# Feed-forward layers with five plain groups ahead of the seven-product ones, the scaled x split chunk by chunk, and x reloaded in eight parts

## The reference

```python
D_MODEL, D_FF, EPS = 1024, 2816, 1e-6

def swiglu_half(x, g_pre, w_gate, w_up, w_down, g_post):
    h = rmsnorm(x, g_pre)
    y = (jax.nn.silu(h @ w_gate) * (h @ w_up)) @ w_down
    return x + 0.5 * rmsnorm(y, g_post)

xp = swiglu_half(xp, *ffn1)
xp, sp = token_mixing(xp, None, None, buf0, s0, mix)
xp = swiglu_half(xp, *ffn2)      # and the same for the sample tokens xs
```

## Time and profile before

| | us |
|---|---|
| median of 3 runs | 1514.76 (1513.25 to 1514.83) |
| profiled execution | 1506.69 |
| its span, first to last instruction | 1504.8 |
| TensorE busy | 1435.8 (95%), 12096 products |
| VectorE busy | 908.2 (60%) |
| ScalarE busy | 611.1 (41%) |
| POOL busy | 194.1 (13%) |
| mean granted clock of TensorE | 0.986 |

### The profile page before, as it was taken

One profiled execution on the slowest core, in us unless ns is written; L12 is line 12 of the kernel. 1 busy time (PEld: TensorE's weight loads), 2 busy tenths in 40 slices (PEclk: granted clock), 3 DMA queues, 4 the chain that ended last, 5 costly groups with the idle time before them and its releaser, 6 DMA issues. The chain is left out here.

```text
span 1504.8 us, 30863 instructions
## 1 busy us (share of the span) xinstructions
PE 1435.8 (95%) x12096; PEld 1316.4 (87%) x12096; DVE 908.2 (60%) x1475; ACT 611.1 (41%) x1054; POOL 194.1 (13%) x185
## 2 busy tenths in 40 slices
PE   7799999999999999999998999989987999999996
PEld 6699999999898888877876887779987999999996
DVE  7999997222656775243566533456378899993224
ACT  5465655222521454211134333342344556553222
POOL 4400000000171000332100220021016000000000
PEclk9899999999999999999999999989999999999998
DMA  4233222422589979999997567837231223324221
GB/s 146 71 112 113 96 101 94 161 96 86 199 293 350 334 243 320 355 333 343 375 331 265 189 221 248 285 127 260 95 128 71 78 92 113 113 84 160 96 96 57
DMA packets 114846, 275.74 MB, mean 183 GB/s; under 512 B 15721, under 2 KB 18410, under 8 KB 113698
## 3 DMA queue, kind: packets, MB, share of 16 engines
q1 hardware_dynamic: 108050, 249.66, 47.7%
q0 software_dynamic: 6240, 23.28, 4.4%
q10 hardware_dynamic: 432, 1.05, 0.2%
HBM read 257.55 MB, written 16.39 MB: 182 GB/s over the span
## 5 line engine op out<-in xcount | busy, mean ns | idle before, releaser
L201 ACT ACTIVATE w_high<-w_raw 128x1024 fp32r<-128x1024 f32 (+1 forms) x93 | 108.0, 1162 | 451.9 <-PE psum L226 406.5
L205 DVE TENSOR_TENSOR w_low<-w_raw,w_high 128x1024 fp32r<-128x1024 f32 (+1 forms) x93 | 126.9, 1365 | 234.2 <-ACT w_high L201 234.2
L1168 PE MATMUL psum<-h_high,gu_high 128*128 128x260 f32 x608 | 173.8, 286 | 6.6 <-DVE h_low L920 5.6
L1169 PE MATMUL psum<-h_low,gu_high 128*128 128x260 f32 x608 | 173.4, 285 | 0.0
L1170 PE MATMUL psum<-h_high,gu_low 128*128 128x260 f32 x608 | 173.0, 284 | 0.0
L1168 PE MATMUL psum<-sums_high,gu_high 128*128 128x260 f32 x456 | 130.5, 286 | 15.7 <-DVE gu_low L992 12.7
L222 PE MATMUL psum<-mix_h_high,w_high 128*128 128x260 f32 x672 | 139.2, 288 | 0.0
L224 PE MATMUL psum<-mix_h_low,w_high 128*128 128x260 f32 x672 | 135.3, 283 | 0.0
L226 PE MATMUL psum<-mix_h_high,w_low 128*128 128x260 f32 x672 | 135.2, 283 | 0.0
L1170 PE MATMUL psum<-sums_high,gu_low 128*128 128x260 f32 x456 | 129.9, 285 | 0.0
L222 PE MATMUL psum<-a_high,w_high 128*128 128x260 f32 x616 | 124.6, 283 | 3.5 <-DVE w_low L205 3.5
(11 more groups left out here) (448 smaller groups left out, 3314.1 us busy)
## 6 DMA issues: line engine op xcount, KB each, us to landing
kv_ring<-in_cache_k SPq DMA_DIRECT2D x256, 256.0 KB, 4.1
kv_ring<-in_cache_v SPq DMA_DIRECT2D x256, 256.0 KB, 3.8
w_raw<-in_w_dn SPq DMA_DIRECT2D x32, 704.0 KB, 4.1
w_raw<-in_w_proj SPq DMA_DIRECT2D x44, 512.0 KB, 6.7
raw_even<-in_w_gu SPq DMA_DIRECT2D x40, 512.0 KB, 4.3
raw_odd<-in_w_gu SPq DMA_DIRECT2D x40, 512.0 KB, 3.7
spill<-h_f POOLq DMA_DIRECT2D x20, 260.0 KB, 5.0
gates<-spill POOLq DMA_DIRECT2D x16, 260.0 KB, 4.4
```

Source lines behind the costliest of these rows:

```text
L201: act.activation(w_high[:, u, 0:nk, :], w_raw[:, u, 0:nk, :], ACT.Copy).then_inc(high_done, 1)
L205: dve.tensor_tensor(w_low[:, u, 0:nk, :], w_raw[:, u, 0:nk, :], w_high[:, u, 0:nk, :].bitcast(F32), ALU.subtract).then_inc(low_done, 1)
L1168: pe.matmul(out, wh[:, slot, :], hi, start=start, stop=False, skip_group_check=True)
L1169: pe.matmul(out, wh[:, slot, :], lo, start=False, stop=False, skip_group_check=True)
```

## The change

- G0 is 5: groups 0 to 4 are plain, 5 to 21 seven-product. The buffers of the plain groups' weights alternate (odd_high and even_high, and so for low), and t4 takes t1's place. `second_products` runs u = 0 to 7.
- POOL's four additions are gone. ScalarE writes the even chunks of xw as x times the weights with four copies behind the factor (`weighted`), and POOL multiplies by the factor. The orders of ScalarE, VectorE and POOL around the start of the seven-product groups are written anew.
- In the last plain half (u = 7) TensorE counts gu_used after every chunk (the "free" units). `token_high(k)` waits for chunk k alone and not for the whole half.
- In the down stage x comes back in eight transfers, of one chunk each, between those of w_dn blocks 3 and 14; the last three go together.

```diff
 SLOTS = 25
 
 
-G0 = 3
+G0 = 5
 NG7 = KF - G0
 
 
 def unit_order():
 
-    order = [("gate", 1), ("up", 1), ("gate", 2), ("up", 2), ("P5", G0), ("PA", G0), ("P6", G0), ("P7", G0)]
+    order = [(kind, c) for c in range(1, G0 - 1) for kind in ("gate", "up")] + [("gate", G0 - 1)]
+    order += [("free", k) for k in range(KD - 1)] + [("up", G0 - 1), ("P5", G0), ("PA", G0), ("P6", G0), ("P7", G0)]
     for n in range(G0 + 1, KF):
         order += [("PA", n), ("P3", n - 1), ("P5", n), ("P6", n), ("P4", n - 1), ("P7", n)]
...
+POOL_STEPS = [("xw", k) for k in range(0, KD, 2)] + [("late", 0), ("t", 0), ("late", 1), ("t", 1), ("t", 2), ("t", 3)]
+POOL_STEPS += [("late", c) for c in range(2, G0)]
 ACT_STEPS, DVE_STEPS = act_steps(), dve_steps()
 ACT_AT, DVE_AT, POOL_AT = [{t: i + 1 for i, t in enumerate(s)} for s in (ACT_STEPS, DVE_STEPS, POOL_STEPS)]
 
...
                     load(4, 0)
                     load(4, 1)
                     for n in range(5, KF):
-                        sp.wait_ge(gu_dve, V("S4", n - 2))
+                        sp.wait_ge(gu_dve, V("S4", n - 2) if n - 2 >= G0 else V("second", 2 * (n - 3) + 1))
                         load(n, 0)
-                        sp.wait_ge(gu_dve, V("P4", n - 2))
+                        if n - 2 >= G0:
+                            sp.wait_ge(gu_dve, V("P4", n - 2))
                         load(n, 1)
 
                     sp.wait_ge(gu_dve, V("P4", LAST - 1))
                     load_block(sp, w_dn, 0, nb, 0, NKD)
                     sp.wait_ge(gu_used, at("PA", LAST))
                     load_block(sp, w_dn, 1, nb + 1, 1, NKD)
-                    sp.wait_ge(gu_dve, V("low", LAST))
-                    sp.dma_start(x[:, :, :], a["x"] if which == 0 else a["x_spill"]).then_inc(x_back, 16)
-                    load_stream(sp, w_dn, 2 * KD, nb, NKD, first=False)
+                    for n in range(2, 2 * KD):
+                        if n == 4:
+                            sp.wait_ge(gu_dve, V("low", LAST))
+                        if n >= 4 and n % 2 == 0:
+                            for k in range(n // 2 - 2, n // 2 - 1 if n < 2 * KD - 2 else KD):
+                                sp.dma_start(x[:, k, :], a["x"][:, k, :] if which == 0 else a["x_spill"][:, k, :]
+                                             ).then_inc(x_back, 16)
+                        load_block(sp, w_dn, n, nb + n, n % 2, NKD)
                     if which == 0:
                         load_first(sp, a["w_proj"], nb + 2 * KD, KD)
                     if store:
...
 
                     def normed(k):
 
-                        pool.wait_ge(gu_pool, G("add", k))
+                        pool.wait_ge(gu_act, A("xg", k))
                         pool.tensor_tensor(xw[:, k, :], xw[:, k, :], factor[:, :], ALU.mult).then_inc(gu_pool, 1)
 
-                    for k in range(0, KD, 2):
-                        pool.wait_ge(h_low_done, m0 + k + 1)
-                        pool.tensor_tensor(xw[:, k, :], h_high[:, k, :].bitcast(F32), h_low[:, k, :].bitcast(F32),
-                                           ALU.add).then_inc(gu_pool, 1)
                     pool.wait_ge(norm_rec, norm_n + 1)
                     for k in range(0, KD, 2):
                         normed(k)
+                    late(0)
                     pool.wait_ge(gu_pool, G("xw", KD - 2))
                     pool.tensor_tensor(t1[:, :, :], xe1, xe2, ALU.subtract).then_inc(gu_pool, 1)
-                    late(0)
+                    late(1)
                     pool.wait_ge(gu_dve, V("xw", KD - 1))
                     pool.wait_ge(gu_pool, G("t", 0))
                     pool.tensor_tensor(t2[:, :, :], xo2, t1[:, :, :], ALU.add).then_inc(gu_pool, 1)
-                    late(1)
                     pool.wait_ge(gu_pool, G("t", 1))
+                    pool.wait_ge(gu_dve, V("t", 0))
                     pool.tensor_tensor(t4[:, :, :], xo1, t2[:, :, :], ALU.subtract).then_inc(gu_pool, 1)
                     pool.tensor_tensor(xe2, xo2, xe2, ALU.subtract).then_inc(gu_pool, 1)
-                    late(2)
+                    for c in range(2, G0):
+                        late(c)
 
                 @block.scalar
                 def _(act):
...
 
                     def second_high(u):
 
-                        if u < 2:
-                            act.wait_ge(gu_in[2 + u], arrived(1))
-                            src = c_raw[:, u, :, :]
-                        else:
-                            act.wait_ge(gu_in[u - 2], arrived(2))
+                        c, m = u // 2 + 1, u % 2
+                        act.wait_ge(gu_in[2 * (c % 2) + m], arrived(c))
+                        if c == 2:
                             act.wait_ge(gu_dve, V("second", 1))
-                            src = raws[0][:, u - 2, :, :]
-                        act.activation(c_high[u // 2][:, u % 2, :, :], src, ACT.Copy).then_inc(gu_act, 1)
+                        elif c > 2:
+                            act.wait_ge(gu_used, at("up", c - 2))
+                        src = c_raw[:, m, :, :] if c == 1 else raws[c % 2][:, m, :, :]
+                        act.activation(c_high[(c - 1) % 2][:, m, :, :], src, ACT.Copy).then_inc(gu_act, 1)
+
+                    def weighted(k):
+
+                        act.activation(xw[:, k, :], x[:, k, :], ACT.Copy, scale=vecs[:, v_pre + k:v_pre + k + 1]
+                                       ).then_inc(gu_act, 1)
                     second_high(0)
                     second_high(1)
                     factor_act(act, norm_n)
...
                         act.activation(h_high[:, k, tok], xw[:, k, tok], ACT.Copy).then_inc(gu_act, 1)
 
                     def unit_high(kind, n):
...
                         act.wait_ge(gu_dve, V("hid2", n))
                         act.activation(a_high[:, n, :], af[:, :], ACT.Copy).then_inc(gu_act, 1)
 
+                    weighted(0)
+                    weighted(2)
+                    weighted(4)
+                    weighted(6)
                     second_high(2)
                     silu(0)
                     second_high(3)
+                    high(0)
                     silu(1)
-                    high(0)
                     sum_high(0, t_hi[:, 0:4, :], t1[:, :, :])
+                    second_high(4)
                     high(1)
+                    second_high(5)
                     sum_high(1, t_hi[:, 4:8, :], t2[:, :, :])
+                    sum_high(2, t_hi[:, 8:12, :], t4[:, :, :])
+                    silu(2)
+                    high(2)
+                    second_high(6)
+                    second_high(7)
                     act.wait_ge(block_used, n0 + 2)
                     unit_high("PA", G0)
                     unit_high("P5", G0)
-                    sum_high(2, t_hi[:, 8:12, :], t4[:, :, :])
                     unit_high("P6", G0)
-                    silu(2)
-                    act.wait_ge(gu_used, at("up", 2))
+                    silu(3)
+                    high(3)
+                    silu(G0 - 1)
+                    act.wait_ge(gu_pool, G("xw", KD - 2))
                     act.wait_ge(gu_dve, V("xw", KD - 1))
                     for k in range(KD):
                         token_high(k)
                     sum_high(3, T3_HIGH, xe2)
-                    high(2)
+                    high(G0 - 1)
                     if which == 1:
-                        act.wait_ge(x_back, 32 + 16 * KD)
+                        act.wait_ge(x_back, 16 + 32 * KD)
                     second_product(G0)
                     unit_high("PA", G0 + 1)
                     for n in range(G0, KF):
...
                     normed(5)
                     normed(7)
                     second_low(3)
-                    gate_scale(1)
                     hidden(0)
                     low(0)
+                    gate_scale(1)
+                    second_low(4)
                     sum_low(0, t_lo[:, 0:4, :], t1[:, :, :], t_hi[:, 0:4, :])
                     hidden(1)
                     low(1)
+                    second_low(5)
+                    sum_low(1, t_lo[:, 4:8, :], t2[:, :, :], t_hi[:, 4:8, :])
+                    dve.wait_ge(gu_act, A("t", 2))
+                    dve.tensor_tensor(t_lo[:, 8:10, :], t4[:, 0:2, :], t_hi[:, 8:10, :].bitcast(F32), ALU.subtract)
+                    if which == 1:
+                        dve.wait_ge(x_back, 16 + 32 * KD)
+                    dve.wait_ge(gu_pool, G("xw", KD - 2))
+                    dve.tensor_tensor(t4_rest[:, :, :], t4[:, 2:4, :], t_hi[:, 10:12, :].bitcast(F32),
+                                      ALU.subtract).then_inc(gu_dve, 1)
+                    gate_scale(2)
+                    hidden(2)
+                    low(2)
+                    second_low(6)
+                    second_low(7)
                     sum_one(G0)
-                    sum_low(1, t_lo[:, 4:8, :], t2[:, :, :], t_hi[:, 4:8, :])
                     unit_low("PA", G0)
                     sum_two(G0)
```

(20 more changed lines are left out.)

79 lines of the change are left out of this document (42 added, 37 removed).

## The result

The changed kernel took 1501.78 us (median of 4 runs, 1500.8 to 1501.87) against 1514.8 (1513.25 to 1515.84) for the kernel before, a ratio of 0.9916 (0.9901 to 0.9932): 13.0 us faster. The prediction was 1502.1. The sum behind it was right in total. Its terms were not: three errors of 1.3 to 2.3 us cancel, which is luck, and this part of the document is mostly about them.

What follows compares the result with a forecast made beforehand. A VectorE, ScalarE and POOL chain was taken to bound the transition, TensorE the rest. Terms 4.9 + 5.7 + 3.5 - 1.5 = 12.6 us took the profiled 1506.69 to 1494.1; 8.1 carried over gave 1502.1, range 1499 to 1505 (58%).

Steps and rivals of the forecast that it cites:

- What bounds the kernel: Transition to seven-product groups: a chain through VectorE, ScalarE and POOL sets P6, 39.1 us behind gate_scale(0); elsewhere TensorE bounds.
- Part 1: Front of each layer: replacing POOL's four additions by ScalarE copies frees VectorE; gains 2.0 and 2.9, together 4.9 us.
- Part 2: Two more plain groups in each of two layers: 48 added TensorE products cost 5.8 us.
- Part 3: New transition order: P6 56.4 us behind gate_scale(0) instead of 59.2; 5.7 us gained in both layers, added products included.
- Clock: Slow products behind gaps near 2.8 us: a fall at P6 in one of two layers costs 1.5 us, bounds 0 and 3.8.
- Part 4: Down stage: reloading x in eight pieces behind w_dn blocks 2 and 3 removes all 3.5 us of TensorE's waits.
- The 8.1 us carried over: Whole kernel: the runs' median lay 8.1 us above the profiled execution; added to 1494.1, it gives 1502.1.
- The stalls come back: Rival, 17%: at the transition, split weights come later than walked by 3 us a layer or more; 1508, up to 1513.
- The front gives nothing: Rival, 8%: at each layer's front, ScalarE's squares or copies are the next limit; gain 7.7, 1507 us.
- The reload was hidden: Rival, 4%: in the down stage, something else hid the reload or its wait moves a block on; gain 9.1, 1505.7.
- The clock stays at half: Rival, 5%: behind the gap before group 4, up to 132 products a layer run slow; kernel ends slower, at 1523.
- Better than the sum: Rival, 8%: loads and hand-overs quicker than priced, no clock falls, group 4's gap shrinks; gain 16 to 20, 1497.

Runs made afterwards that it cites:

- the kernel with the early second_high(6): The changed kernel with second_high(6) and second_low(6) moved ahead of sums 1 and 2: 1499.56 us, ratio 0.9896.
- copies alone: The kernel before with POOL's four additions replaced by ScalarE's four scaled copies, nothing else: 1511.37 us, ratio 0.9974.
- after: The changed kernel with the whole change, against the kernel before, as first measured and profiled: 1501.78 us, ratio 0.9916.
- after again: The changed kernel, unchanged, measured and profiled once more on another comparison's chip: 1500.31 us, ratio 0.9895 to the kernel before.
- the kernel whose tokens wait: The changed kernel where every token_high waits for the whole last plain half, not its own chunk: 1499.68 us, ratio 0.9896.
- reload alone: The kernel before with x reloaded in eight parts, nothing else: 1509.71 us, ratio 0.997.
- the reordered one: The changed kernel with the steps of ScalarE, VectorE and POOL re-ordered around the transition: 1492.43 us, ratio 0.9842.

## Why the prediction was right, and where it was not

The size came out right by errors that cancel and by a difference carried over unexplained; the mechanism of the transition, which is most of the prediction, was right within 1 us a layer. Against the kernel before as profiled again, stretch by stretch (us gained):

| stretch | predicted | measured |
|---|---|---|
| to zero, first layer (part 1) | 2.0 | 3.3 |
| zero to down, first layer (parts 2 and 3, clock) | 2.1 | 1.1 |
| down stage, first layer (part 4) | 2.0 | 3.8 |
| mixer | 0 | -0.5 |
| merged to zero (part 1) | 2.9 | 2.9 |
| zero to down, second layer (parts 2 and 3, clock) | 2.1 | 0.8 |
| down stage, second layer (part 4) | 1.5 | 1.8 |
| sum | 12.6 | 13.2 |

- **What bounds the kernel.** Right. Its reading that TensorE's speed doesn't set P6 is borne out by the kernel with the early second_high(6): a gap of 2.70 less, and P6 no earlier.
- **Part 1.** The second layer's 3 x 0.98 was exact, with and without the other parts. In the first layer 3.3 came where 2.0 was counted. The copies alone gave 1.8, with ScalarE's root waiting 1.93 us for TensorE's sums, which is 0.40 in after. The difference of 1.5 is TensorE's, as shown with the copies alone: it is the next limit, as predicted, but how soon it comes to full speed differs from execution to execution and decides whether the part is worth 1.8 or 3.3. The prediction had no term for it. The four meetings were put at 4.4 us; VectorE's sums end 3.6 earlier in after than in the first profile (24.9 to 21.3).
- **Part 2.** The products are 12144 where they were 12096, the 48 added. Their time cannot be seen by itself. That the four gaps and the distance of P6 all fit a walk which has the added products at 5.75 a half speaks for it.
- **Part 3.** The walk put P6 at 56.4 and it came at 57.2. The gaps are in the right places and right within 0.25 us, but the walk runs early: by 0.4 at the second half of group 3, 0.6 at group 4, 0.9 at PA. "The walk met the old order within 0.1" was a poor warrant: it says nothing of another order. The prices were taken from that order's own rows, and in the new order the errors of a longer walk add up. That is 1.6 us in both layers together. The step of the release chunk by chunk was given no price of its own, rightly: it has none.
- **Clock.** Mis-sized: 1.5 us for one of two layers, against 1.2 in each of two, 2.4. It is not the same every time. Behind a gap of 2.55 or 2.56 it fell in both layers of after and of after again, and in neither of the kernel whose tokens wait. The bounds of 0 and 3.8 hold all of this.
- **Part 4.** Both waits went, 3.5 us, as predicted, and there is no new wait behind them. Another 2.0 came that no row of the first profile could give, mostly the fall of the clock behind the 2.0 us wait. The prediction's 7.0 against 8.9 was no comparison: 7.0 is the median of one piece, 8.9 the whole. The eight pieces took 4.5 us each to land in the first layer and 4.6 in the second. The Trainium skill (SBUF — State Buffer, Summary: rules for kernel authors) has one transfer and not several where the transfer bounds. Nothing here waits for x, so the trace of after cannot tell which is faster; it shows that it does not matter off the path.
- **The 8.1 us carried over.** This decided whether the prediction was right. They are the mixer's (6.9 of the 8.4 between the two profiles, 6.1 of it at the stalls) and the clock's in the down stage (1.5). Without them the forecast would have been 1494.1, 7.7 us too low. The change touches nothing of the mixer, and the stalls stay in after. The fall in the down stage went with its wait, and that is why part 4 was worth more. Carrying a difference between profile and median over without knowing what it is was a guess; a change to the mixer could have broken it. That it held is luck.
- **Rivals.** "The stalls come back" is refuted with 3 us a layer, but 0.8 of it is true. "The front gives nothing" is refuted in after, and nearly true in the first layer of the old order, where 1.8 us gained were 1.7 lost behind zero. "The reload was hidden" is refuted by the reload alone. "The clock stays at half" is refuted: no slow stretch behind group 4's gap has more than 20 products. "Better than the sum" did not come in the changed kernel; the reordered one shows that the time was there.

## What to carry to other kernels

Walk a chain of engines from one zero, and predict distances from it and not times: P6's distance repeated within 0.3 us between the layers and executions of one order, while spans of one kernel moved by 8. A change that lets an engine start earlier than it can use (the tokens chunk by chunk) is seen in the timeline before it is written: look at what stands ahead of the first released step on the same engine. Where a chain through other engines is the bound, filling TensorE's gap moved it to the next one here, and the order of the chain's own steps brought it in, by 4.9 us a layer.

## What the runs showed of the hardware

- TensorE stopped in the middle of a block with nothing that released it, two to six times within five microseconds, for up to 1.6 us at a time. It happened at the start of the mixer in 9 of 10 profiles, each time beginning 31.5 to 33.5 us behind the mixer's first product, with a fall of the clock in it or behind it in 8 of the 9, and cost 5.6 to 7.1 us. In after VectorE and ScalarE were busy for half a microsecond each of four meanwhile, and the transfers were down to 33 GB/s. What causes it was not tried and stays open.
- The granted clock fell to half behind most of the gaps of 2.5 to 2.8 us in the feed-forward layers, and not behind all: after one of 2.71 it did, after one of 2.70 in the same place of the other layer it did not, and in the kernel whose tokens wait it fell behind none of four. It also fell behind shorter ones: 1.79 before P6 with the reload alone, in both layers, and the wait of 2.0 in the down stage in two of the three executions of the old order that have it. Behind P6 a fall costs ten to twelve products at 0.22 us, 1.2 us.
- Group 0's products came to full speed at 12.3 us in one execution and at 15.4 in another, with the same orders up to there, and TensorE ended them 1.5 us apart.
